# The chain of a bidirectional RWKV-7 layer: next tile's staging, Gram products and block inverse placed half a slot ahead, a second buffer for the removal products, the group norm half a tile sooner

## What is computed

```python
def rwkv7_scan(r, w, k, v, kk, a, s0):
    def step(s, inp):
        r_t, w_t, k_t, v_t, kk_t, a_t = inp
        s_kk = einsum('bhvk,bhk->bhv', s, kk_t)
        s = (s * w_t[:, :, None, :] - s_kk[..., None] * (kk_t * a_t)[:, :, None, :]
             + v_t[..., None] * k_t[:, :, None, :])
        return s, einsum('bhvk,bhk->bhv', s, r_t)
...
for d, f in enumerate((_ident, _flip)):
    yc_d, s_ctx = rwkv7_scan(f(rc), f(wc), f(kc), f(vc), f(kkc), f(ac), s0)
    yl_d, _ = rwkv7_scan(f(rl), f(wl), f(kl), f(vl), f(kkl), f(al), s_ctx)
...
y = head_groupnorm(ys[0] + ys[1], ln_g, ln_b) + bonus
return (y * g) @ wo
```

## Time and profile before

| | us |
|---|---|
| median of 3 runs | 3733.2 (3730.28 to 3734.76) |
| profiled execution, its own time | 3732.19 |
| its span, first to last instruction | 3730.4 |
| chain of layer 0, from its first `W` to the last copy | 295 to 708 |
| chain of layer 3 | 3061 to 3456 |
| mean granted clock of TensorE | 0.974 of full |

### The profile page before, as it was taken

How to read it: one execution, slowest core, us unless ns; L and a number is a source line. 1 busy time by engine, 2 the same in 40 slices (tenths; PEclk the granted TensorE clock), 3 DMA queues, 4 the chain that set the end, 5 groups by cost and what they waited for, 6 DMA issues and landing times. The chain is left out here.

```text
span 3730.4 us, 73707 instructions
## 1 busy us (share of the span) xinstructions
PE 3504.9 (94%) x28645; PEld 2559.6 (69%) x28645; DVE 2487.6 (67%) x4480; ACT 1160.5 (31%) x2478; POOL 449.7 (12%) x737
## 2 busy tenths in 40 slices
PE   7987888999999999999999999999999978888999
PEld 2447777588877454555887866588875547677887
DVE  7975655389998666663898954489977845554431
ACT  3034554133301434421332024223302134553210
POOL 2012223000000323220000000000001012221000
PEclk9998999999999999999999999999999988998999
DMA  6641011144443333223443520144343611111454
GB/s 208 203 132 22 16 22 22 36 136 133 125 146 100 100 99 102 80 77 98 132 128 118 162 71 26 37 138 131 121 129 113 207 45 22 23 20 27 121 152 133
DMA packets 583542, 365.03 MB, mean 98 GB/s; under 512 B 125376, under 2 KB 552712, under 8 KB 581160
## 3 DMA queue, kind: packets, MB, share of 16 engines
q1 hardware_dynamic: 556776, 250.40, 24.2%
q0 software_dynamic: 26432, 110.07, 8.4%
HBM read 348.73 MB, written 11.67 MB: 97 GB/s over the span
## 5 line engine op out<-in xcount | busy, mean ns | idle before, releaser
L274 PE MATMUL PS<-H,WR 128*128 128x512 f32 (+1 forms) x1424 | 477.0, 494 | 0.0
L2490 PE MATMUL PS<-WORK 64*64 64x64 f32 (+2 forms) x6944 | 378.2, 240 | 77.0 <-DVE WORK L3074 59.4
L567 DVE SCALAR_TENSOR_TENSOR WORK<-WORK,SC 128x512 f32<-128x512 f32 x616 | 418.4, 746 | 0.7
L274 PEld LDWEIGHTS PS<-H,WR 128*128 128x128 f32 x1424 | 268.0, 190 | 187.3 <-issue 167.2
L2490 PEld LDWEIGHTS PS<-WORK 64*64 64x64 f32 (+1 forms) x6944 | 296.8, 147 | 127.5 <-issue 61.7
L1450 PE MATMUL PS<-BIG,WR 128*128 128x512 f32 (+1 forms) x944 | 329.2, 502 | 5.2 <-DMA WR<-in_rw_wo_dram 2.1
L547 POOL DMA_DIRECT2D WORK<-in_ada_w_dram x88 | 66.4, 755 | 1845.8 <-DVE WORK L567 873.8
L2767 ACT ACTIVATE WORK<-PS 128x64 f32<-128x64 f32 (+2 forms) x528 | 163.4, 327 | 399.7 <-PE PS L2490 323.5
L1450 PEld LDWEIGHTS PS<-BIG,WR 128*128 128x128 f32 x944 | 176.0, 190 | 133.8 <-issue 112.7
L988 ACT ACTIVATE WORK<-PS 128x512 f32<-128x512 f32 x252 | 135.1, 541 | 343.3 <-PE PS L921 302.1
L921 PE MATMUL PS<-BIG 128*128 128x256 f32 x984 | 223.9, 380 | 0.0
(11 more groups left out here) (354 smaller groups left out, 6310.6 us busy)
## 6 DMA issues: line engine op xcount, KB each, us to landing
WORK<-in_ada_w_dram POOLq DMA_DIRECT2D x88, 1024.0 KB, 6.1
WR<-in_ffn_w_in_dram SPq DMA_DIRECT2D x220, 256.0 KB, 2.9
BIG<-in_ffn_w_in_dram SPq DMA_DIRECT2D x132, 256.0 KB, 3.3
WR<-in_ffn_w_out_dram SPq DMA_DIRECT2D x106, 256.0 KB, 2.8
WR<-in_ssd_w_in_dram SPq DMA_DIRECT2D x96, 256.0 KB, 2.8
BIG<-scratch_dram POOLq DMA_DIRECT2D x8, 2048.0 KB, 8.0
BIG<-in_ffn_w_out_dram SPq DMA_DIRECT2D x36, 256.0 KB, 3.2
BIG<-in_ada_w_dram SPq DMA_DIRECT2D x4, 2048.0 KB, 18.2
```

What stands on the lines that cost most here:

```text
L274: mm = pe.matmul(outs, WR[:, slot, k, 0:m], rhs(k), start=first and k == 0, stop=last and k == nk - 1)
L567: lag(vec.scalar_tensor_tensor(ACC3[:, s_], w, by, ACC3[:, s_], ALU.mult, ALU.add), label)
L2490: return pe.matmul(o, lhs, rhs, start=start, stop=stop)
```

## The change

Nothing is added to or taken from the arithmetic; what changes is the list of steps, and two buffers.

- Staging of tile i+1 from `L01` to `ad1`, with `ar0` and `ar1`, now stands in slot 2i (k = 0 to 14; `ar0` at k = 10, `ar1` at 12). In slot 2i+1 follow `pct` to `BVv`. `kf` and the table load `TS` stand at the end of the odd slot before.
- `GT` i+1 s moves from k = 12 and 14 of slot 2i+1 to k = 0 and 8; `IB` i+1 from the start of slot 2i+2 to k = 9 of slot 2i+1.
- `E` i 0 moves from k = 19 of slot 2i to k = 9 and its levels from 20, 21, 23, 24 to 10, 12, 14, 16 (tile 0 keeps its places). `R` and `H` move behind it.
- P1 to P3 of tile i-1 stand in slot 2i+1, where those of tile i-2 stood in slot 2i+2.
- The removal products are written to `ADS[n % 2]`, two buffers. `INV` holds the inverses alone; the turned copies lie in `TURN`, one half at a time, so `E` ends in two transposes of 128x256 where one of 128x512 stood.
- The waits follow the new order. `rates` and its wait are untouched, and `AR` keeps its two buffers.

```diff
-            for k, step in ((2, ("R", i, s)), (3 - 2 * s, ("H", both[0], s)), (6 - 3 * s, ("H", both[1], s))):
-                early.append((k, *step))
-            late.append((5, "Rv", i, s))
-            at = (20, 21, 23, 24) if s == 0 else (2, 4, 6, 8)
-            early.append((at[0] - 1, "E", i, s))
+            at = ((10, 12, 14, 16) if i else (20, 21, 23, 24)) if s == 0 else (2, 3, 5, 6)
             early += [(at[n // 2], *step) for n, step in enumerate(levels)]
             if s == 0:
-                early.append((0, "IB", i))
+                if i == 0:
+                    early += [(0, "IB", 0), (0, "kf", 1), (0, "TS", 1)]
+                early += [(6, "R", i, 0), (8, "H", both[0], 0), (11, "H", both[1], 0), (at[0] - 1, "E", i, 0)]
...
-            elif more:
-                early += [(12, "GT", i + 1, 0), (14, "GT", i + 1, 1)]
...
+            else:
+                early += [(0, "E", i, 1), (2, "R", i, 1), (4, "H", both[0], 1), (7, "H", both[1], 1)]
+                late.append((5, "Rv", i, 1))
+                if more:
+                    early += [(0, "GT", i + 1, 0), (8, "GT", i + 1, 1)]
+                    late += [(k, n, i + 1) for k, n in (
+                        (3, "pct"), (5, "pr1a"), (6, "pr2a"), (8, "pr1b"), (9, "pr2b"), (9, "IB"), (10, "bsum"), (11, "bs"),
+                        (12, "sd0"), (13, "sd1"), (14, "VT"), (18, "BV"), (20, "BVv"))]
+                if i + 2 < KD:
+                    late += [(18, "kf", i + 2), (20, "TS", i + 2)]
+                if i:
+                    late += [(k, n, i - 1) for k, n in ((9, "P1"), (11, "P2"), (13, "P2e"), (14, "P2v"), (16, "P3"))]
```

More of the change, by code:

```diff
@@ L2313, in program @@
         AR = [H[:, 2048 * n:2048 * n + 2048].rearrange("p (d n t) -> p d n t", d=2, n=2) for n in range(2)]
-        AD, SD, SIG, AA, PN = (both_d(T) for _ in range(5))
+        AD0, SD, SIG, AA, PN = (both_d(T) for _ in range(5))
         ARS = work(2048).rearrange("p (d n t) -> p d n t", d=2, n=2)
@@ L2590, in grams_k @@
                     cs = tok(ORDER_Q[d][4 * s + c])
-                    for n, src in enumerate((AD, SD)):
+                    for n, src in enumerate((ADS[i % 2], SD)):
                         for hs in HALF:
@@ L2623, in x_step @@
                         if d:
-                            last = mm(blocks_of(out, n), ZB[d][hs, c, :], second(d, n)(INV[hs, d, 0, 4 * s + c, :]))
+                            last = mm(blocks_of(out, n), ZB[d][hs, c, :], second(d, n)(INV[hs, d, 4 * s + c, :]))
                         elif n < 32:
-                            last = mm(blocks_of(out, n), INV[hs, d, 1, 4 * s + c, :], second(d, n)(ZB[d][hs, c, :]))
+                            last = mm(blocks_of(out, n), TURN[hs, d, c, :], second(d, n)(ZB[d][hs, c, :]))
                         else:
-                            last = mm(out, INV[hs, d, 1, 4 * s + c, :], ZB32[d][hs, c, :])
+                            last = mm(out, TURN[hs, d, c, :], ZB32[d][hs, c, :])
                 done(last, f"{q}.xy{s}{m}")
@@ L2652, in chain_u @@
                 for hs in HALF:
-                    last = mm(PS[hs, d, Q:P], INV[hs, d, 0, c, :], WS[d][hs, :])
+                    last = mm(PS[hs, d, Q:P], INV[hs, d, c, :], WS[d][hs, :])
                 done(last, f"{q}.u{c}")
@@ L3069, in expand @@
                         vec.wait_ge(pe_done, C.at(f"{t}.{2 * i - 2 + d}.u{4 * s_ + 3}"))
-                    dst = INV[:, d, 1 - d, 4 * s_:4 * s_ + 4, :].rearrange("p c (b j) -> p c b j", j=BLK)
-                    lag(vec.tensor_tensor(dst, XBS[:, s_, d].unsqueeze(2).broadcast_to([P, 4, 4, BLK]), keep, ALU.mult))
+                    dst = INV[:, d, 4 * s_:4 * s_ + 4, :] if d else TURN[:, d, :, :]
+                    lag(vec.tensor_tensor(dst.rearrange("p c (b j) -> p c b j", j=BLK), XBS[:, s_, d].unsqueeze(2).broadcast_to([P, 4, 4, BLK]), keep, ALU.mult))
                 vec_last()
-                half = lambda x: x[:, :, 4 * s_:4 * s_ + 4, :].rearrange("p d c f -> p d (c f)")
-                lag(vec.transpose(half(INVX[:, 0:4:3]), half(INVX[:, 1:3])), f"{t}.{i}.xi{s_}")
+                flat = lambda x: x.rearrange("p c f -> p (c f)")
+                inv, turned = (flat(INV[:, d, 4 * s_:4 * s_ + 4, :]) for d in range(2)), [flat(TURN[:, d]) for d in range(2)]
+                lag(vec.transpose(next(inv), turned[0]))
+                lag(vec.transpose(turned[1], next(inv)), f"{t}.{i}.xi{s_}")
             def grams_r(i, s_):
@@ L3099, in x_step @@
                     vec_last()
-                    both = lambda h: INV[:, :, h, 4 * s_:4 * s_ + 4, :].rearrange("p d c f -> p d (c f)")
-                    lag(vec.transpose(both(1), both(0)), f"{t}.{q}.xx{s_}{m}")
+                    flat = lambda x: x.rearrange("p d c f -> p d (c f)")
+                    lag(vec.transpose(flat(TURN), flat(INV[:, :, 4 * s_:4 * s_ + 4, :])), f"{t}.{q}.xx{s_}{m}")
             def chain_u(q, c):
```

71 lines of the change are left out of this document (30 added, 41 removed), and 6 rows, old and new, of the table at.

## The result

The changed kernel took **3794.4 us** (median of 4 runs, 3791.22 to 3795.78) against 3731.7 for the kernel before beside it (3727.69 to 3734.76): slower, by a ratio of 1.0167, 95% interval 1.015 to 1.0185. The forecast was 3790, range 3750 to 3830. The profiled execution has a span of 3794.0 us. TensorE does the same 28645 matmuls; its busy time is 18 us longer than in the earlier trace rows, so the same matmuls took longer.

A forecast was written before the change was run, and what follows sets the result against it. TensorE, 94% of the span, bounds the kernel; only the two chains change. Layer 0 +26.2 and layer 3 +30.5, together +56.7 on 3732.2, give 3788.9, with the runs' median 1 us above: 3790 us, range 3750 to 3830.

The forecast's parts named there:

- staging of tile 0: Staging of the first tile, its removal products one unit earlier under 7 us of matmuls per unit: costed at nothing.
- start, to the second load of blocks: Tile 1's first Gram groups come earlier in the chain: -7.4 us in layer 0, -6.8 in layer 3.
- first beat: First round, block load to block load: 57.6 + 1.5 against 49.9, +9.2 us, in layer 0; +5.7 in layer 3.
- five beats: Five later tile rounds: 57.6 against 53.3 us each in layer 0, +21.5; 57.0 against 51.6 in layer 3, +27.0.
- end: Tile 7's last three chunks come after the wait for `Z` they filled before: +2.9 us layer 0, +4.6 layer 3.
- The rates: First Gram groups, tiles 2 to 7, wait for rates released by y7, the last chain step: 4.8 us, layer 3 3.7.
- The clock at the border: TensorE's clock falls to half behind the two waits for the rates, costing 1.8 us a tile.
- Stretch A: From the end of the second Gram group to first level `Z`: 24.6 us, the floor from the inverse's round trip.
- stretch B: From `Z` to the end of the next second Gram group: 26.4 us in layer 0, 25.5 in layer 3, without rates.
- Layer 3's wait of 5 us ahead of `Z`: The chain reaches `Z` in some 19.5 us, so TensorE waits 5 us; another 1.4 a tile for the clock.
- No hindrance: Rival: rates do not delay the Gram group, since y7 comes early enough or exponentials still decide; 3717 us, chance 0.09.
- near-no-change case: Rival: the rates' wait exists but stretch B's other stalls go and the round trip shortens; 3726 to 3740 us, chance 0.05.

The follow-up runs named there:

- sooner rates: Changed kernel; GpSimd makes both removal rates once the old tile's last `W` has read the buffer, first Gram group waits for these alone: 3731.8 us, ratio 1.0007.
- sooner expansion: On top of the sooner rates, the expansion of the even slot at k = 6 on VectorE instead of 9: 3714.3 us, ratio 0.996.

## Why the forecast held, and which steps failed

The sum against what was measured. A group of the last chain step gives the end of each layer's chain; TensorE of the kernel before:

```profile
708.81 0.33 PE L2490 MATMUL PS<-WORK,BIG 64*64 64x64 f32 x4
...
3456.21 0.33 PE L2490 MATMUL PS<-WORK,BIG 64*64 64x64 f32 x4
```

and the same groups in the changed kernel:

```profile
748.70 0.33 PE L2493 MATMUL PS<-WORK,BIG 64*64 64x64 f32 x4
...
3519.84 0.33 PE L2493 MATMUL PS<-WORK,BIG 64*64 64x64 f32 x4
```

| term, us | layer 0 forecast | measured | layer 3 forecast | measured |
|---|---|---|---|---|
| staging of tile 0 | 0 | +6.5 | 0 | 0 |
| start, to the second load of blocks | -7.4 | -9.1 | -6.8 | -7.2 |
| first beat | +9.2 | +9.4 | +5.7 | +7.7 |
| five beats | +21.5 | +30.3 | +27.0 | +20.8 |
| end | +2.9 | +2.8 | +4.6 | +5.5 |
| sum | +26.2 | +39.9 | +30.5 | +26.8 |

The staging's 6.5 is the shift of the first `Z` of tile 0, 287.70 to 294.15; in both layers the start is the shift of the load of tile 1's blocks without the shift there already was. The end is what the groups above moved by beyond the last beat. Between the two chains the changed kernel won 3.1 us back, at one wait in a layer that the change does not touch. TensorE of the kernel before:

```profile
2110.20 5.81 PE L1195 MATMUL PS<-WORK 128*128 128x256 f32 x18 [3.16 <-DVE WORK L1044]
```

and of the kernel before with doubled rates:

```profile
2118.39 4.12 PE L1195 MATMUL PS<-WORK 128*128 128x256 f32 x18 [0.52 <-DVE WORK L1044]
```

In the changed kernel it is 0.17, and in no other traced kernel over 1.1, so the 3.16 most likely belong to that one execution and not to the change. 39.9 - 3.1 + 26.8 is 63.6, for 63.6 between the two spans.

**The rates: right.** GpSimd starts within 0.2 us of y7, both halves of the group wait, TensorE's whole slot stands behind them, six times a layer. The forecast had 4.8 + 1.8 for wait and clock, 6.6 us a tile in layer 0. The sooner rates lowered the beat by 5.3. What they leave or bring, 0.5 us of wait for the rates in every tile and 1.65 in one of five, is 0.8 a tile, so the rates' own cost lies between 5.3 and 6.1, a little under the forecast. In layer 3 it was 3.7 + 1.8 = 5.5, and 4.8 came back. The two waits were to be some 2.5 us each and are 2.70 and 1.56. The rates ran near their short side, as expected.

**The clock at the border: right.** 1.8 was forecast, and filling the wait gave back 1.5 in layer 0 and 1.3 in layer 3, net of the low clock that then stood behind more of the `Z`.

**Stretch A failed.** The step was: "So A has a floor of 24.6 that the order cannot lower", and the forecast then put A at that floor. In layer 0 A is 26.9 to 27.2 us in tiles 2 to 6, on average 2.4 more, and in layer 3 25.2 to 27.2, on average 1.6 more. The round trip was what was forecast: from the copies of the Gram group to the landed inverse 21 to 24 us in both kernels. But I took the landing as the moment at which the expansion runs, and did not look at what stood ahead of it on VectorE in the new order: a Gram mask, the chain copy of chunk 5, the product of keys. With the expansion ahead of these, A was 24.0 to 25.4 in layer 0. With that and the rates' wait both gone the beat is 51.3 us in layer 0 and 50.1 in layer 3, where the forecast's tile without rates had been 24.6 + 26.4 = 51.0 and 24.6 + 25.5 = 50.1. So stretch B, too, was sized right.

**Layer 3's wait of 5 us ahead of `Z` failed with it.** It was derived from a chain that reaches `Z` 5 us before the inverse is ready. It was 2.4 to 2.5 in tiles 1 to 6, mostly the product of keys and the expansion (0.68 and 1.63 us) behind a chain copy. A low clock did follow, in four of six tiles, but three of the six had had it in the kernel before, so 1.4 us a tile were not added. In layer 0, where the forecast had no clock term behind `Z`, three tiles had it. All of the beat but A took 32.3 us in layer 0 (forecast 26.4 + 4.8 + 1.8 = 33.0) and 29.6 in layer 3 (25.5 + 3.7 + 3.2 = 32.4). So in layer 0 A's 2.4 prevailed and five beats were put 9 us too low, and in layer 3 it was more than made up: by the 1.4 of clock, by the rates (taken up to 0.7 too high) and by some 0.7 that stays open. So five beats were put 6 too high there.

**The staging of tile 0, "costed at nothing", failed.** The 7 us of matmuls per unit were there. But the removal products ran beside GpSimd now, 1.58 us each for 0.69 before, and the bonus sum went to a unit in which six partial sums stand ahead of it. I had named the cover on TensorE and not looked at VectorE's row. Putting the order back made layer 0 shorter by 8.0 us in the trace, while the medians leave the gain open.

**How much was luck.** The mechanism that decides, the rates behind y7, was right and near its size. That the total came within 5 us of the measured one was in part luck: 6.5 for the staging and 9 for layer 0's beats were missing from the sum, while layer 3's beats were 6 too high, the start won 2 more than forecast, and 3 came back between the layers at a wait that the change does not touch.

**The rivals.** "No hindrance", 3717, needs the rates ready before y7: the sooner rates with the sooner expansion make that case, and it is 3714.3. The changed kernel with the sooner rates alone is the near-no-change case, 3731.8 against 3726 to 3740, but got there by another way than that rival's.

## What to carry to other kernels

When work is moved ahead by a part of a loop's round, look at each buffer it writes: a write on an idle engine that was free before may now be released by the last step of the round, and what stands behind it at the head of the next round is the whole engine. Split such a write by its readers, or put the waiting group a few steps into the round; the kernel with either was as fast as the kernel before (ratios 1.0007 and 1.0003). And where an in-order engine turns a landed transfer into work, its time is the landing only if nothing of the new order stands ahead of it there.

## What the runs showed of the hardware

Adding 64 matmuls a tile to the waits made the kernel 19.9 us faster (17 by the ratios), and the granted clock stayed at 1.00 behind them; ahead of the 0.50 in the changed kernel TensorE had stood still for 2.70 and 1.56 us, with 1.1 us of matmuls between. A low clock is not the same in every round: behind the wait of 2.4 to 2.5 us ahead of `Z` it was 0.50 to 0.73 in some tiles and 1.00 in others of the same layer.

A GpSimd product and a VectorE product, both with two inputs on the chip, slow each other: a product of 512 columns on VectorE took 0.68 to 0.69 us alone and 1.57 to 1.75 beside GpSimd, the expansion 1.63 alone, 2.70 beside the removal rates and 3.7 in the one slot where the read rates ran beside it too. The Trainium skill states it as a rule (SBUF — State Buffer, Who interferes with whom: a VectorE instruction with two SBUF inputs contends with a GpSimd instruction that reads SBUF), and the trace agrees. The kernel before lost 20 us when its rates were doubled, with no wait of TensorE for the rates anywhere; how much of the 20 is this contention is not shown.
